# RWKV stage: added unit-matrix products in TensorE's order of a decoder step

## What is computed

```python
kk = kk / jnp.maximum(jnp.sqrt(jnp.sum(kk * kk, axis=-1, keepdims=True)), 1e-12)
def step(S, inp):
    r_t, d_t, k_t, v_t, kk_t, a_t = inp
    sa = jnp.einsum('bhvk,bhk->bhv', S, kk_t)
    S = S * d_t[:, :, None, :] - sa[..., None] * (kk_t * a_t)[:, :, None, :] + v_t[..., None] * k_t[:, :, None, :]
    return S, jnp.einsum('bhvk,bhk->bhv', S, r_t)
mu, var = mean and variance of y over a head
yn = (y - mu) * lax.rsqrt(var + GN_EPS) * lnx_w + lnx_b
bonus = jnp.sum(r * k * r_k, axis=-1, keepdims=True) * v
return (yn + bonus) * g
```

## Time and profile before

| | |
|---|---|
| Runs | 3728.3, 3740.2, 3741.31 us |
| Profiled execution | 3746.3 us, span 3744.6 us from the first to the last instruction |
| PE busy over the span | 3360.3 us (90%) |
| VectorE (DVE) busy | 2967.9 us (79%) |
| ACT, GpSimd busy | 1145.5 us (31%), 1616.8 us (43%) |
| Mean granted TensorE clock over the span | 0.931 |

### The profile page before, as it was taken

The page is one execution under the profiler, slowest core; times in us unless marked ns, Lnnn a source line. Parts: engine busy times, 40 slices in busy tenths (PEclk is TensorE's granted clock), DMA queues, the critical chain, the costliest instruction groups (busy, mean ns, idle before and its releaser), DMA issues.

```text
span 3744.6 us, 62834 instructions
## 1 busy us (share of the span) xinstructions
PE 3360.3 (90%) x21215; PEld 3117.5 (83%) x21215; DVE 2967.9 (79%) x6155; ACT 1145.5 (31%) x2174; POOL 1616.8 (43%) x1414
## 2 busy tenths in 40 slices
PE   7998848888897998848779999999999999999997
PEld 7998736777777755547779999999999999999997
DVE  6543655465553589989889999999999999999998
ACT  3101443333331122359822222222222222222222
POOL 2120001111110134420077776667777676676674
PEclk9999767778887999979989999999999999999998
DMA  3222330000004000015599999999999999999996
GB/s 122 97 87 78 110 105 6 22 34 13 1 10 150 23 26 33 19 60 224 217 358 356 357 349 346 346 356 357 353 356 360 352 356 343 336 361 350 350 355 214
DMA packets 296943, 781.46 MB, mean 209 GB/s; under 512 B 28376, under 2 KB 129240, under 8 KB 295424
## 3 DMA queue, kind: packets, MB, share of 16 engines
q0 software_dynamic: 135568, 493.54, 35.8%
q1 hardware_dynamic: 161264, 286.56, 21.4%
HBM read 709.32 MB, written 70.11 MB: 208 GB/s over the span
## 4 chain that ended last, share of the span: by engine, by line
PE 30%; DVE 9%; issue 7%; DMA 6%; POOL 2%; DVEq 1%; ACT 1%; POOLq 0%; ACTq 0%; SPq 0%
PE experts_down_ps L113 7%; PE experts_down_ps L115 7%; PE experts_down_ps L114 7%; DMA stream_u<-in_up_rows,experts_u_at 4%; PE experts_up_ps L114 3%; PE experts_up_ps L115 3%; PE experts_up_ps L113 3%; DMA stream_u<-in_down,experts_v_at 2%; DVE stream_u L3388 2%; DVE stream_h_rows_of L3405 2%; POOL stream_u L3144 1%; DVE stream_h L3411 1%; DVE picking_mean_square L2919 1%; DVE stream_h_rest L2919 1%; POOL stream_u L3129 1%
## 5 line engine op out<-in xcount | busy, mean ns | idle before, releaser
L3129 POOL DMA_INDIRECT stream_u<-in_up_rows,experts_u_at x448 | 599.2, 1338 | 312.3 <-DVE experts_dot L3388 145.2
L3144 POOL DMA_INDIRECT stream_u<-in_down,experts_v_at x448 | 592.1, 1322 | 246.7 <-issue 98.2
L113 PE MATMUL experts_up_ps<-experts_u_hi,experts_up_hi 128*128 128x320 f32 x2048 | 634.8, 310 | 30.9 <-DVE experts_up_lo L3359 24.6
L113 PE MATMUL experts_down_ps<-experts_act_hi,experts_down_hi 128*128 128x320 f32 x2048 | 639.6, 312 | 23.3 <-DVE stream_h L3411 16.9
L114 PE MATMUL experts_down_ps<-experts_act_lo,experts_down_hi 128*128 128x320 f32 x2048 | 635.6, 310 | 0.0
L115 PE MATMUL experts_down_ps<-experts_act_hi,experts_down_lo 128*128 128x320 f32 x2048 | 635.3, 310 | 0.0
L114 PE MATMUL experts_up_ps<-experts_u_lo,experts_up_hi 128*128 128x320 f32 x2048 | 634.2, 310 | 0.0
L115 PE MATMUL experts_up_ps<-experts_u_hi,experts_up_lo 128*128 128x320 f32 x2048 | 634.1, 310 | 0.0
L3405 DVE SCALAR_TENSOR_TENSOR stream_h_rows_of<-stream_u,experts_weight,stream_h_rows_of 128x1024 f32<-128x1024 f32 x448 | 567.9, 1279 | 31.8 <-DMA stream_u<-in_down,experts_v_at 20.7
L3388 DVE CUSTOM_DVE_ANT_0 stream_u<-stream_u,stream_u_rows_of 128x1024 f32<-128x1024 f32 x448 | 544.9, 1216 | 41.2 <-DMA stream_u<-in_up_rows,experts_u_at 41.1
L113 PEld LDWEIGHTS experts_down_ps<-experts_act_hi,experts_down_hi 128*128 128x128 f32 x2048 | 386.9, 189 | 31.5 <-DVE stream_h L3411 23.6
(11 more groups left out here) (466 smaller groups left out, 6172.9 us busy)
## 6 DMA issues: line engine op xcount, KB each, us to landing
stream_h_rest<-in_up SPq DMA_DIRECT2D x128, 512.0 KB, 7.2
stream_u<-in_down_pieces SPq DMA_DIRECT2D x128, 512.0 KB, 6.3
gates<-spread_spread SPq DMA_DIRECT2D x10, 4096.0 KB, 11.5
experts_gates<-gates SPq DMA_DIRECT2D x64, 640.0 KB, 9.6
cols<-inp_done POOLq DMA_DIRECT2D x26, 576.0 KB, 3.8
inp_w_in<-in_w_in SPq DMA_DIRECT2D x27, 512.0 KB, 4.4
pick_w_query<-in_w_query SPq DMA_DIRECT2D x14, 512.0 KB, 3.8
stream_u<-in_up_rows,experts_u_at POOLq DMA_INDIRECT x448, 7.0
```

The lines of the kernel that those rows point to most:

```text
L113: pe.matmul(out, w_hi, x_hi, start=start, stop=False)
L3129: pool.indirect_dma_start((half_row if i == HALF_DOT else u_row[b]), None, up_rows_d, bass.IndirectOffsetOnAxis(ap=u_at[slot][:, col:col + ...
L3144: pool.indirect_dma_start((half_row if i == HALF_ADD else v_row[b]), None, v_table, bass.IndirectOffsetOnAxis(ap=v_at[slot][:, col:col + 1 ...
```

## The change

The tensor engine's program gets a product whose result nobody reads: the unit matrix `eye` times up to 512 columns of `masks`, a constant. It is written to chain_ps, or to turn_ps[1] where chain_ps is in use. It stands ahead of these waits of TensorE: the bonus thirds of pair 0 (slots 4 to 6), unit_rows at steps 10 to 12 and the bonus thirds at steps 18, 20 and 22 of the later pairs, start_from_samples (256 columns, pairs 1 to 3), and the third mean of all four pairs. Where the bank could still have a reader, a wait for that reader stands ahead of the product: for y of the tiles before (y_ready), or for the mask of from_k (fk_ready). In the third mean the wait for y_ready moves ahead of the one for `side["free"]`. Nothing is taken out, and the other engines' programs are the same. These are 28 products, 25 of 512 and 3 of 256 columns.

```diff
                 side = {"free": (zeroed, 1)}
+                spare_cols = masks[:].rearrange("p a b t -> p (a b t)")
+
+                def keep_busy(ps, n):
+
+                    pe.matmul(ps[:, 0:n], eye[:], spare_cols[:, 0:n], start=True, stop=True)
+
+                def keep_busy_beside(step, j):
+                    slot = step % MERGE_SLOTS + 1
+                    group = GROUPS[(j - 1) * GROUP_COUNT + step // MERGE_SLOTS + 1]
+                    before = GROUPS[group.i - 1]
+                    if slot in (2, 3, 4):
+                        pe.wait_ge(fk_ready, group.i + 1)
+                        keep_busy(turn_ps[1], BANK)
+                    else:
+                        pe.wait_ge(y_ready, before.ci if slot == 1 else before.ended())
+                        keep_busy(chain_ps, BANK)
@@ prepare
                     if UNIT_AT <= step < UNIT_AT + 3:
                         c = step - UNIT_AT
+                        keep_busy_beside(step, j)
                         pe.wait_ge(*side["free"])
@@
                     if step in BONUS_STEPS:
+                        keep_busy_beside(step, j)
                         pe.wait_ge(prep_vec, reached(PREP_DVE, j, "weighted"))
@@
                 def start_from_samples(group):
+                    if group.i:
+                        pe.wait_ge(y_ready, GROUPS[group.i - 2].ended())
+                        keep_busy(chain_ps, BANK // 2)
                     pe.wait_ge(*side["free"])
@@ mean
                     if c < 2:
                         pe.wait_ge(fk_ready, min((j + 1) * GROUP_COUNT + 1, len(GROUPS)))
+                        pe.wait_ge(y_ready, j * NT + 3 * c + 3)
                     else:
+                        pe.wait_ge(y_ready, j * NT + 3 * c + 3)
+                        keep_busy(chain_ps, BANK)
                         pe.wait_ge(*side["free"])
-                    pe.wait_ge(y_ready, j * NT + 3 * c + 3)
                     pe.matmul(stat_ps[c], head_pair[:], thirds(y_of[j % 2], c), start=True, stop=True).then_inc(ep_pe, 1)
```

## The result

| | before | after |
|---|---|---|
| Runs, median of four | 3739.5 us (3728.3 to 3741.3) | 3709.5 us (3707.9 to 3709.9) |
| Ratio, 95% interval | 1 | 0.9918 [0.9904, 0.9933] |
| Profiled execution: span | 3744.6 us | 3707.5 us |

The change makes the kernel 0.8% faster, about 31 us by the ratio (25 to 36 by its interval). The forecast was 18 us, with 3722 us in a range of 3702 to 3746 us. (The median of before is 3739.5 us with a fourth run of 3738.8 us.)

The account below looks back on a forecast made before the run. TensorE's low clock, some 260 us of the RWKV stage, was taken as the bound. Gains of 25 us less 6.4 us of costs gave about -18.5 us: 3722 us on the median, range 3702 to 3746 us.

Parts of the forecast that it names:

- What bounds the stage: RWKV stage: TensorE's low clock, some 260 us at 1.2 GHz, is the resource; all its waits are a few tens of microseconds.
- Price of a product: Each added 512-column product takes 0.85 us at full clock, 1.71 us at half; half of that for 256 columns.
- Cover: Existing TensorE waits hide most products; uncovered ones, mainly six at steps 20 and 22 (5.1 us), cost 6.4 us in all.
- Gain behind steps 12 and 18: Ends of third and fourth groups: six slow stretches at full clock save 25.5 us, taken as 21.5 us.
- the sixth stretch: Behind steps 12 and 18: only five in six stretches counted, because stretches shift and a lull may lie differently.
- The slope of 0.2: Check from two whole first chain groups: 2.9 us for some 14 us of low clock; six stretches would give 13 us.
- First pair: Long low stretch after finish_first: 2.9 us, 60% held, gain 1.7 us; products there cost 0.2 us.
- Not touched: Falls behind the first group's solve wait and behind row_norms go on, shifting some 3 us per pair either way.
- The first rival: TensorE's short waits: clock falls only after an idle window, so filling them holds nothing and only costs remain; chance 0.17.
- rival A: All added products: they hold nothing, so +6 to +12 us, 3746 to 3752 us; chance 0.17.
- Rival B: Covered waits: what ends them is itself queued behind the products, so the cover fails; 3763 us, chance 0.06.
- Rival C: All six stretches hold and neighbouring lulls, some 20.5 us ones included, are saved too; about -35 us, 3705 us, chance 0.11.

Follow-up runs that it names:

- e1: The changed kernel with each of the 28 added products cut to 2 columns; 3742.8 us, ratio 1.0002.
- e9: e4 without the ten products of step 10, step 11 and the third means; 3693.1 us, ratio 0.9878.
- e7: e3 with 256 columns instead of 512 in each of its six products; 3718.1 us, ratio 0.9945.
- e8: The changed kernel without the three products of finish_first; 3712.9 us, ratio 0.9918.
- e4: e2 plus two 512-column products ahead of the solve wait ending a pair's first group (three pairs); 3693.5 us, again 3686.5 us.
- e6: e4 with one more 512-column product ahead of row_norms (step 6, three pairs); 3693.0 us, ratio 0.9869.
- e10: e4 with a product ahead of the last pair's first mean and none in the tail; 3678.8 us, ratio 0.9830.
- e3: The changed kernel with only the six products of steps 12 and 18 left of 28; 3717.6 us, ratio 0.9938.
- e2: The changed kernel without the six products of steps 20 and 22; 3704.5 us, ratio 0.9900.

## Why the prediction was right, and where it was off

- What bounds the stage. Right: the low clock behind lulls is the resource, not the waits. e1 keeps every wait and instruction and has the time of before. I read the waits too small, however: PE is idle for 98 us of the stage (620 less 521.95), not for a few tens. The argument does not hang on it, since filled waits gave nothing by themselves.
- Price of a product. Right: 0.85 us forecast, 0.86 us measured at each of the six uncovered places and 0.86 us taken from the waits of step 18 and of the third means. The six waits of steps 11 and 12 lost 0.73 us in the mean, since two of them stood behind work at half clock before.
- Cover. Right at steps 11, 12, 18 and the third means of three pairs: shorter waits, same end. At step 10 the traces show it in the first of the three pairs, where PE's wait for neg_x is 2.36 us before, 1.51 us after and 2.37 us in e9, which has no product there.
- Gain behind steps 12 and 18. The mechanism was right and the term too small: 21.5 us forecast, 30.3 us in the trace. Of the 8.8 us, 4 us are the sixth stretch that I had given up without a row for it (the sum went by five of six; here all six held, in e7 with 256 columns five). The rest is size: the stretches came down to 6.2 and 5.5 us, not 6.6 and 5.9 (2.6 us; my yardstick, the last pair's 5.9 us, has 0.18 us of idle time in it, and why the rest of it is longer I didn't find out), and the steps ahead of them gained 2.2 us that I had not counted. The slope of 0.2, which I took for a check downwards, compared two unlike groups: 133 PE instructions with 2.7 us of idle time against 124 with 0.7 us. The same group of 124 went from 27.8 us at 0.71 to 22.0 us at 0.91, which by the same arithmetic is 5.8 us for some 12 us of low clock, a slope of 0.48.
- First pair. I wrote 1.7 us, the trace showed 7.3, the runs of e8 against the changed kernel some 3 us with open cause.
- Not touched. Right in that both kinds of fall went on, too small in size: I allowed some 3 us a pair, and the ends of the first groups moved by -2.6, +8.9 and -1.7 us. That they and the second groups' -3.7 us add up to only +1 us is luck. e4 then showed that the first of the two can often be held, e6 that one product ahead of row_norms held it in one pair of three.
- The first rival, and the rule behind it. No wait of PE ahead of the falls behind steps 12 and 18 was longer than 2.4 us, and the clock fell in all six places; in the changed kernel it fell in none of them, and with products of 2 columns (e1) again in all six. So filling these short waits did hold the clock, and rival A, at 0.17, did not come. The Trainium skill, "TensorE: Matmul & The Clock Gate", "What's actually happening", lets the clock fall after an idle window; read as plain idle time, as I read it in the prediction, the traces do not agree with it.
- Rival B fell: no covered wait ended later for the product. Rival C was nearer to the measurement than my forecast (3705 and 3722 us against 3709.5 us, which is also just under the 3710 us where the forecast case began). Of its reasons one came, that all six stretches hold; the 20.5 us stretches were not saved, and what made up for them was the size of the terms and the first pair.
- What it showed in the profile: stage shorter by 33.5 us instead of 18, clock 0.86 as forecast. By the two means some 260 us of the stage were at half clock before and some 165 us after, so each microsecond of low clock that went gave back about 0.35 us; the forecast had 18 us for nearly the same change of the clock. That the clock came out right while the time was too small is therefore luck in part.

## What to carry to other kernels

Where TensorE runs a latency-bound order, look for PE-bound stretches at half clock and for the lull ahead of each; here a product without a reader cost nothing in a wait longer than itself and paid in what ran behind it (six such products made 23 us, with those at the further waits of e10 some 60 us). Place them by the wait in the trace, and leave them out where there is no wait: there they cost their full 0.86 us. Since falls shift with everything else, judge by several runs and not by one trace, and look at the stage apart from the rest of the kernel: a stretch that was spared in one kernel can cost 9 us in the next.

## What was unexpected of the hardware

Fp32 transposes held the clock behind steps 12 and 18 as products did (ratio 0.9915 against 0.9918). The same instructions up to the same time can be followed by a low stretch of 7 us (e8) or of 20 us (before, e1, e3, e7). And the later stages, with the same instructions in every kernel, took from 2578.1 to 2593.8 us, as much of a spread as most of the differences that the experiments look for. The changed kernel's four runs lie within 2 us, but that filled lulls make the times steadier is not shown: the runs of e2 lie 20 us apart, those of e4 and e9 15 us.
